# Output stage of a hybrid encoder layer: the turn, router and affinity work of each tile moved one tick later

## The reference

```
h = RMSNorm(x)*(1+scale1)+shift1
x = x + gate1 * RMSNorm(W_out [mLSTM heads | 2-D neighbourhood-attention heads](h W_in))
h = RMSNorm(x)*(1+scale2)+shift2
x = x + gate2 * RMSNorm(expert-choice SwiGLU MoE(h))

# the router, inside the expert-choice MoE
aff = softmax(h @ w_router)            # 16 experts
gate, idx = top_k(aff.T, 128)          # each expert takes its 128 best tokens
```

## Time and profile before

| | |
|---|---|
| median of 3 runs | 2409.93 us (2409.59 to 2413.72) |
| profiled execution: its own time | 2409.95 us |
| profiled execution: span, first to last instruction | 2408.2 us |
| mean granted TensorE clock | 0.987 |
| TensorE busy | 2301.4 us (96%), 13,589 matmuls |
| VectorE, ScalarE, GpSimd busy | 1207.3 us, 1103.9 us, 606.8 us |

### The profile page before, as it was taken

The page is one execution under the profiler, slowest core; times in us unless marked ns, Lnnn a source line. Parts: engine busy times, 40 slices in busy tenths (PEclk is TensorE's granted clock), DMA queues, the critical chain, the costliest instruction groups (busy, mean ns, idle before and its releaser), DMA issues. The chain is left out here.

```text
span 2408.2 us, 35208 instructions
## 1 busy us (share of the span) xinstructions
PE 2301.4 (96%) x13589; PEld 1920.2 (80%) x13589; DVE 1207.3 (50%) x1881; ACT 1103.9 (46%) x1828; POOL 606.8 (25%) x676
## 2 busy tenths in 40 slices
PE   6999999999999998999957999999999999999997
PEld 4679989777899897677746888888888888888886
DVE  3222334654323345665566455544545556666665
ACT  4223444655433335665443444444444455555552
POOL 3004332443133424530021011111010122222434
PEclk9999999999999999999988999999999999999998
DMA  8835455658464559764446566666656678888785
GB/s 316 259 108 182 145 162 185 189 149 192 113 200 134 175 172 237 219 179 169 160 190 263 201 218 211 225 218 215 203 205 228 220 261 315 320 308 290 284 300 175
DMA packets 239039, 511.49 MB, mean 212 GB/s; under 512 B 36980, under 2 KB 128004, under 8 KB 235824
## 3 DMA queue, kind: packets, MB, share of 16 engines
q1 hardware_dynamic: 190960, 394.78, 48.6%
q0 software_dynamic: 47936, 114.77, 16.0%
HBM read 415.32 MB, written 93.69 MB: 211 GB/s over the span
## 5 line engine op out<-in xcount | busy, mean ns | idle before, releaser
L2489 DVE TENSOR_TENSOR moe_w_lo<-moe_wf,moe_w_hi 128x2048 fp32r<-128x2048 f32 x192 | 439.4, 2292 | 455.4 <-ACT moe_w_hi L2364 454.1
L2364 ACT ACTIVATE moe_w_hi<-moe_wf 128x2048 fp32r<-128x2048 f32 x192 | 367.8, 1916 | 549.1 <-PE moe_acc L2626 549.0
L2626 PE MATMUL moe_acc<-moe_w_hi,moe_x_hi 128*128 128x512 f32 x1024 | 401.7, 392 | 0.9 <-DVE moe_x_lo L2495 0.6
L2626 PE MATMUL moe_acc<-moe_w_hi,moe_x_lo 128*128 128x512 f32 x1024 | 398.9, 390 | 0.0
L2626 PE MATMUL moe_acc<-moe_w_lo,moe_x_hi 128*128 128x512 f32 x1024 | 398.5, 389 | 0.0
L2626 PEld LDWEIGHTS moe_acc<-moe_w_hi,moe_x_hi 128*128 128x128 f32 x1024 | 192.3, 188 | 40.4 <-DVE moe_x_lo L2495 0.8
L2626 PEld LDWEIGHTS moe_acc<-moe_w_hi,moe_x_lo 128*128 128x128 f32 x1024 | 192.2, 188 | 40.3
L2626 PEld LDWEIGHTS moe_acc<-moe_w_lo,moe_x_hi 128*128 128x128 f32 x1024 | 192.4, 188 | 38.9
L1790 PE MATMUL banks<-fr_w_hi,fr_h_hi 128*128 128x256 f32 x768 | 223.2, 291 | 0.0
L1790 PE MATMUL banks<-fr_w_lo,fr_h_hi 128*128 128x256 f32 x768 | 217.0, 283 | 0.0
L1790 PE MATMUL banks<-fr_w_hi,fr_h_lo 128*128 128x256 f32 x768 | 217.0, 282 | 0.0
(11 more groups left out here) (294 smaller groups left out, 4096.9 us busy)
## 6 DMA issues: line engine op xcount, KB each, us to landing
moe_wf<-in_w_expert_gate SPq DMA_DIRECT2D x64, 1024.0 KB, 5.0
moe_wf<-in_w_expert_up SPq DMA_DIRECT2D x64, 1024.0 KB, 4.9
moe_wf<-in_w_expert_down SPq DMA_DIRECT2D x64, 1024.0 KB, 6.5
fr_w_raw<-in_w_units SPq DMA_DIRECT2D x28, 1024.0 KB, 6.8
fr_bias<-in_na_bias SPq DMA_DIRECT2D x16, 1520.0 KB, 11.1
fr_a_w<-in_w_ada POOLq DMA_DIRECT2D x16, 1024.0 KB, 8.2
scratch_qk_t<-fr_stage SPq DMA_DIRECT2D x64, 256.0 KB, 2.5
scratch_vov<-fr_stage SPq DMA_DIRECT2D x96, 128.0 KB, 2.3
```

The costliest lines, as they stand in the source:

```text
L2364: nc.scalar.activation(w_hi[:, q, :, :], wf[:, q, :, :], ACT.Copy).then_inc(w_hi_ready, 1)
L2489: nc.vector.tensor_tensor(w_lo[:, q, :, :], wf[:, q, :, :], w_hi[:, q, :, :].bitcast(F32), ALU.subtract).then_inc(w_lo_ready, 1)
L2626: mm = nc.tensor.matmul(acc[:, j, b, :], x[:, g, k, :], w[:, q, a, h * HALF:(h + 1) * HALF], start=(k == 0 and i == 0), stop=(k == KC - 1 ...
```

## The change

In all ticks of tiles 2 to 15 the work on tile t-2 stands one tick later. On TensorE the two turns go from u0 and u2 to u1 and u3, the router from u4 to u5, the turned affinities and the sum from u6 to u7. On ScalarE `turn_out` goes from u1 and u3 to u2 and u4, `take_parts` from u5 to u6, and `take_aff` and `powers` from u7 to u0 of the next tile, behind `take_y` and its square. VectorE's `logits` goes from u6 to u7. SyncE's store of the affinities goes from u7 to u3 of the next tile. ScalarE's order in the two tiles after the last product is that of before. `keep_awake`, which issues filling transposes in the tail, moves with its neighbours.

```diff
@@ SyncE
-                    if 0 <= t - 3 < TT:
-                        sp.wait_ge(aT_ready, t - 2)
-                        sp.dma_start(aff_view[t - 3], affT[:, :]).then_inc(aff_stored, 16)
+                    if 0 <= t - 4 < TT:
+                        sp.wait_ge(aT_ready, t - 3)
+                        sp.dma_start(aff_view[t - 4], affT[:, :]).then_inc(aff_stored, 16)
@@ ScalarE
                 for t in range(N_TILES + OUT_TAIL):
+                    steady = t < N_TILES
                     if 1 <= t <= N_TILES:
                         take_y(t - 1, 1)
                         out_squares(h2[:, (t - 1) % 2, :], 0, (1,))
+                    if 4 <= t <= N_TILES:
+                        take_aff(t - 4)
+                    if 3 <= t <= N_TILES:
+                        powers(t - 3)
                     if t == TT:
                         split_mix(TT, (1,))
                     yield
-                    if 2 <= t <= N_TILES + 1:
+                    if not steady and t <= N_TILES + 1:
                         turn_out(t - 2, 0)
                     yield
                     if t == 0:
                         split_o(4)
+                    if steady and t >= 2:
+                        turn_out(t - 2, 0)
                     yield
                     if t == 0:
                         split_o(5)
-                    if 2 <= t <= N_TILES + 1:
+                    if not steady and t <= N_TILES + 1:
                         turn_out(t - 2, 1)
...
+                    if steady and t >= 2:
+                        turn_out(t - 2, 1)
...
-                    if 2 <= t <= N_TILES + 1 and t != N_TILES:
+                    if t == N_TILES + 1:
                         take_parts(t - 2)
                     yield
                     if t == 0:
                         split_mix(1)
-                    yield
-                    if t >= 3:
+                    if steady and t >= 2:
+                        take_parts(t - 2)
+                    yield
+                    if not steady:
                         take_aff(t - 3)
-                    if 2 <= t <= N_TILES + 1:
-                        powers(t - 2)
+                        if t <= N_TILES + 1:
+                            powers(t - 2)
                     yield
@@ VectorE
-                    if 2 <= t <= N_TILES + 1 and t != N_TILES:
+                    if t == N_TILES + 1:
                         logits(t - 2)
                     yield
+                    if 2 <= t < N_TILES:
+                        logits(t - 2)
                     yield
@@ TensorE
                         if 2 <= t <= N_TILES + 1:
-                            if u in (0, 2):
+                            if u in (1, 3):
                                 turn_h2(t - 2, u // 2)
-                            elif u == 4:
+                            elif u == 5:
                                 route(t - 2)
-                        if u == 6 and t >= 3:
+                        if u == 7 and t >= 3:
                             turn_aff(t - 3)
-                        if u == 6 and 2 <= t <= N_TILES + 1:
+                        if u == 7 and 2 <= t <= N_TILES + 1:
                             add_parts(t - 2)
-                        if t == N_TILES and u in (0, 4, 6):
-                            keep_awake(PS, {0: 9, 4: 14, 6: 20}[u])
-                        if t == N_TILES + 1 and u in (0, 2):
+                        if t == N_TILES and u in (1, 5, 7):
+                            keep_awake(PS, {1: 9, 5: 14, 7: 20}[u])
+                        if t == N_TILES + 1 and u in (1, 3):
                             keep_awake(PS, 4)
```

## The result

| | median us | runs | ratio to before |
|---|---|---|---|
| before | 2409.76 | 4 (2408.66 to 2413.72) | |
| changed | 2434.62 | 4 (2432.39 to 2440.97) | 1.0108, 95% interval 1.0095 to 1.0122 |
| forecast | 2432.5 | range 2422 to 2441 | |

The change makes the kernel 1.1% slower. The profiled execution took 2435.86 us with a span of 2434.1 us, 25.9 us more than the span before. Lines of the changed kernel are numbered 14 higher in TensorE's part; attention's are 14 higher in VectorE's and 12 in ScalarE's. Out_y is L1872, the turns L1890, the router L1900, the turned affinities L1908, the sum L1914, attention's turn(n-1) L1963 and product(n-1) L1974.

What follows compares the result with a forecast made beforehand. TensorE was taken as the bound, busy 96% of the span. New waits 28.5, old waits -7.5, tile 8 -1.6, tail +0.6 and clock +2.5 gave +22.5 us on 2409.95: 2432.5 us, range 2422 to 2441.

Steps and rivals of the forecast that it cites:

- the tiles of the stream alone: Tiles 8 to 15: ScalarE is half idle without exponentials, so the shift costs nothing and the tiles keep their pace.
- A: Rival: ScalarE is early enough, moved steps find copies ready and old waits go; 2401.5 us, chance 0.06.
- B: Rival: new waits are absorbed because attention's slots wait for VectorE or DMA; 2405 to 2414 us, chance 0.05.
- the old waits: TensorE's waits in overlapped tiles: ScalarE releases all but one; 7.5 us of them go away.
- D: Rival, half a shift: first turns don't wait, the other three steps do; 2422.3 us, chance 0.08.
- The four steps: Overlapped tiles: first turn waits 2.2 us, second turn 1.4, router 1.65, affinities and sum 1.1; together +28.5 us.
- The handover: From the end of ScalarE's copy to the start of TensorE's waiting instruction: 0.05 us.
- The second turn of tile 2: Second turn costed at 1.4 us wait; slots of tiles 2 to 6 taken as the same work, tile 6 for all.
- The clock: Half-clock stretches behind first-turn waits in tiles 4 to 6, one or two at 1.7 us: +2.5 us, bounds 0 and 5.
- Rival C: The clock falls behind every wait of 1.6 us or more: 13.6 us in place of 2.5; 2443.6 us, chance 0.09.
- Tile 8: Wait for tile 8's input goes as its load no longer follows the affinity store: -1.6 us, bounds -1.7 and +0.6.
- the tail: After tile 15's last product, take_aff and powers come ahead of the first copy: +0.6 us, bounds 0 and +1.7.

Runs made afterwards that it cites:

- late_alone: Kernel before with the late placement from tile 8 on only, old placement in tiles 0 to 7: 2408.85 us, ratio 0.9999.
- affcopy_u7: Changed kernel with ScalarE's take_aff alone put back into u7: 2426.73 us, ratio 1.0074.
- even_ahead_after: Changed kernel with ScalarE's even tick ahead of attention's copy of turn(n-1) and exponentials, in the second request's slots: 2389.68 us, ratio 0.9923.
- late_overlap: Kernel before with the late placement in tiles 0 to 7 only, the old one from tile 8 on: 2433.79 us, ratio 1.0111.
- after_again: The changed kernel itself, run again on the same chip as the repeated filling-transposes run: 2435.15 us, ratio 1.0108.
- store_only: Kernel before with SyncE's store of the affinities alone moved from u7 to u3 of the next tile: 2408.29 us, ratio 0.9998.
- fill_in: Changed kernel with 16 filling transposes ahead of the first turn in tiles 4, 5 and 6: 2430.56 us, ratio 1.0090.
- fill_in_again: Changed kernel with the 16 filling transposes in tiles 4 to 6, repeated beside the changed kernel on one chip: 2429.39 us, ratio 1.0084.

## Why the prediction was right

**Which part decides.** Right: the tiles of the stream alone keep their 13.0 us, and the half of the change that lies there is worth nothing that can be measured (late_alone). Of the rivals in the prediction, A and B fall with the 19 waits themselves: the copies do come behind TensorE, and its waits elsewhere do not shrink. The one for fr_sc stays at 1.0 us; it is the line that the earlier trace rows leave out, and with it ScalarE is the releaser of all but two of the old waits, not of all but one:

```profile
PE banks L1949 <- DVE fr_sc L1619: 1.0, 1, 1.0
```

D is the kernel of affcopy_u7, 8 us under the changed one, and the first turns do wait.

**The new waits.** The four steps were costed at 2.2, 1.4, 1.65 and 1.1 us and wait 2.3, 1.4, 1.6 and 1.0 us; 28.5 us in sum against 29.6 measured, and the 7.5 us of old ones went. The handover, taken as 0.05 us for all four, is 0.25 us behind the affinity copy (4.26 to 4.51), which accounts for the 0.1 us missing from the first turn, and 0.14 us behind the copy ahead of the second turn. The account by places in the slot holds because ScalarE's first work there is the copy of the turn that TensorE has just made (affcopy_u7 takes one of the four away by its order alone, even_ahead_after all of them).

**One wait was mis-sized.** The second turn of tile 2 waits 2.69 us, not 1.4. In the changed kernel's timeline of that slot:

```profile
986.80 0.66 ACT L1271 ACTIVATE fr_sc<-fr_sc,fr_nmax 128x440 f32<-128x440 f32 x1 [1.15 <-DVE fr_nmax L1623]
988.82 0.63 PE L1890 MATMUL banks<-fr_ident,fr_h 128*128 128x128 f32 x4 [2.69 <-ACT fr_h2T L1110]
```

ScalarE's exponential waits 1.15 us for VectorE there. It is the slot after one in which both engines split the next pair's q and k (slots 4, 12 and 20, that is tiles 0, 2 and 4). The prediction had these slots as all of the same work and let tile 6, which has no such split, stand for all; that sentence was wrong. In the changed kernel tile 4 is spared although it has the split too, as its first turn waits 2.3 us; with that wait gone it shows (2.86 us in affcopy_u7).

**The clock** is the term that was too small: +2.5 us forecast with an upper bound of 5, and in the profiled execution it is about 7.3: 5.8 us in tiles 4 to 6 by the filling transposes, and 1.5 us in tile 2, which takes 30.54 us in the changed kernel with its slow stretch and 29.04 us in late_overlap, where none followed. I had counted one or two slow stretches of some 3.4 us at 1.7 us each, and there were four, one of them twice as long, at about 1.5 us for each 3.4 us. The second trace of the same kernel (after_again) has three, none doubled: tiles 2 to 7 take 167.13 us there (979.40 to 1146.53) instead of 169.95, so its clock term is 4.5 us. Rival C, with a slow stretch behind every wait of 1.6 us, goes too far: none of the router's five was followed by one.

The Trainium skill (TensorE: Matmul & The Clock Gate, section HAM oscillation — how this bites in real kernels) tells of a kernel whose waits are longer than the work between them, and whose clock falls at every wait. That is not this kernel: its waits are at most 2.7 us long and the work between them lasts 5 us or more, so the passage gives no reason to expect a fall behind all 19. Here the clock fell behind four of them in one trace and three in the other.

**Tile 8 and the tail.** -1.6 us was forecast for tile 8 and it is -2.0; +0.6 for the tail and it is +0.7. The reason given for tile 8 is right (store_only removes that wait by the store alone), though store_only also shows that the gain isn't safe: there it comes back as another wait.

**The sum.** 22.1 us more of waits and 7.3 us of clock make 29.4 us where tiles 2 to 7 lost 28.65; the 0.75 us between them are not traced. Add -2.0 us for tile 8, +0.7 for the tail, -1.1 for the slow stretch that only the kernel before had ahead of tile 2, and -0.3 in the experts, which nothing explains, and the span grew by 25.9 us. The forecast was 2.1 us under the median. Its direction and its waits came out of the account; that it lay so close is in part luck, as a clock term too small by 4.8 us in this execution, by 2.0 us in the second, and a wait too small by 1.25 us were partly balanced by terms that it didn't have. The second trace shows how much the start alone can do: its tile 2 begins 2.7 us later than in the first, ahead of all that the change touches, and with 2.8 us less in tiles 2 to 7 its time is the same, 2435.36 us. The bounds of the forecast were also added up 1 us too low: 2430.0 - 2 and 2430.0 + 4 + 5 give 2428 to 2439, not 2427 to 2438.

## What to carry to other kernels

When two strands share an engine, look not at how many ticks lie between a copy and its use, but at what stands between them in the program of the engine that copies: here moving maker and user together by one tick kept the distance on paper and put four instructions of attention ahead of the copy. Line the two engines' timelines up on the instruction that they both hang on, and read off who arrives first. And try the order of the helping engine before that of the bound one: in the kernel before, one line moved on ScalarE gave 18 us, the rearrangement of the four steps cost 25.

## What the runs showed of the hardware that was not expected

In the overlapped tiles the traces of this case have 16 waits of TensorE of 2.3 to 2.9 us. Twelve of them were followed by granted clock 0.50 for 3.4 us, in two cases for 6.8 us: four of four in the profiled changed kernel, three of four in its second trace (after_again), two of two in affcopy_u7, two of four in late_overlap, the one that is left in fill_in, and not the one that is left in fill_in_again, though the waits are as long. The router's and the sum's waits of 1.0 to 1.6 us never were. Ahead of tile 2, where the change does not reach, the nine traces of kernels with ScalarE's old order have 15 waits of 1.9 to 2.0 us, and 5 were followed by such a stretch, the one of the earlier trace rows among them.

The same program therefore differs from run to run: tile 5 of the changed kernel takes 32.99 us with a stretch of 6.8 us and 30.12 us with none, and the kernel's four runs took 2432.4 to 2441.0 us at mean granted clocks from 0.987 to 0.983. The kernel without these waits (even_ahead_after) took 2388.3 to 2391.1 us.
